# An attention stage that goes from one query tile to the next without a pause between them

## What is computed

```python
def blocked_attention(q, k, v, scale):
    ...
        s = jnp.einsum('bhgqd,bhgkd->bhgqk', qblk.astype(jnp.float32), kf) * scale
        p = jax.nn.softmax(s, axis=-1)
        return jnp.einsum('bhgqk,bhkv->bhgqv', p, vf)

def odd_attend(q_c, k_c, v_c, q_d, k_d, v_d, lam_p, lam_init, subln_g, w_out):
    o_c = blocked_attention(q_c[:, :, None], k_c[:, :, None], v_c, (NOPE_C + ROPE_C) ** -0.5)[:, :, 0]
    o_d = blocked_attention(q_d, k_d, v_d, DH_D ** -0.5)
    ...
    o_d = rms_norm(o_d[:, :, 0] - lam * o_d[:, :, 1], subln_g) * (1.0 - lam_init)
    return jnp.concatenate([from_heads(o_c), from_heads(o_d)], axis=-1) @ w_out
```

## Time and profile before

| | |
|---|---|
| median of three runs | 1700.18 us (1693.54 to 1701.67) |
| the profiled execution | 1704.54 us |
| its span, first to last instruction | 1702.8 us |
| mean granted TensorE clock | 0.891 of full speed |
| busy: PE, DVE, ACT, POOL | 79%, 31%, 20%, 10% of the span |
| layer 1: attention's units, projection, start of the expert weights | 1164.5 to 1303 us, to 1354.6 us |

### The profile page before, as it was taken

The page is one execution under the profiler, slowest core; times in us unless marked ns, Lnnn a source line. Parts: engine busy times, 40 slices in busy tenths (PEclk is TensorE's granted clock), DMA queues, the critical chain, the costliest instruction groups (busy, mean ns, idle before and its releaser), DMA issues.

```text
span 1702.8 us, 38641 instructions
## 1 busy us (share of the span) xinstructions
PE 1347.7 (79%) x16696; PEld 912.1 (54%) x16696; DVE 525.0 (31%) x1181; ACT 339.7 (20%) x702; POOL 165.9 (10%) x242
## 2 busy tenths in 40 slices
PE   4978859988998579489977748977788939986783
PEld 2457724457878244379844424444455429973441
DVE  1233331235444343411101014545455440111013
ACT  2132201032222102200100013433443220100001
POOL 1012310013333000100000012010000010000001
PEclk9999969999999779689999988986789959999997
DMA  9664162320000550949999966114330185999995
GB/s 384 258 201 138 51 249 99 148 100 3 3 3 4 209 206 0 373 157 398 391 396 403 407 244 250 50 64 149 111 137 1 60 338 216 398 392 396 395 417 190
DMA packets 42713, 357.00 MB, mean 210 GB/s; under 512 B 5755, under 2 KB 10699, under 8 KB 24272
## 3 DMA queue, kind: packets, MB, share of 16 engines
q1 hardware_dynamic: 21456, 302.11, 44.8%
q0 software_dynamic: 9312, 30.85, 5.6%
q10 hardware_dynamic: 11808, 22.03, 4.1%
HBM read 323.95 MB, written 31.01 MB: 208 GB/s over the span
## 4 chain that ended last, share of the span: by engine, by line
PE 65%; DMA 19%; DVE 8%; issue 3%; ACT 3%; SPq 1%; POOL 1%; ACTq 0%; DVEq 0%; POOLq 0%
PE PB L622 59%; DMA arena<-in_w_moe 14%; PE PB L625 5%; DVE arena L1783 5%; DMA ring<-in_w_mod 3%; ACT arena L1366 1%; DMA arena<-expert_out,rows_i 1%; DVE arena L1790 1%; POOL dispatched L565 1%; DMA arena<-in_rw_g 1%; DVE small L1796 1%; DMA dispatched<-arena,rows_i 1%; SPq L398 0%; DMA arena<-dispatched 0%; DVE x L1783 0%
## 5 line engine op out<-in xcount | busy, mean ns | idle before, releaser
L622 PE MATMUL PB<-arena 64*64 64x64 f32 (+6 forms) x9378 | 481.7, 299 | 95.0 <-DMA arena<-in_w_moe 39.5
L622 PEld LDWEIGHTS PB<-arena 64*64 64x64 f32 (+3 forms) x9378 | 377.4, 132 | 187.0 <-issue 80.0
L622 PE MATMUL PB<-ring,hT 128*128 128x512 f32 (+1 forms) x720 | 316.3, 596 | 6.2 <-DVE hT L1786 3.6
L622 PE MATMUL PB<-ring,arena 128*32 128x256 f32 (+2 forms) x3648 | 215.4, 392 | 35.8 <-DMA ring<-in_w_moe 34.3
L622 PEld LDWEIGHTS PB<-ring,hT 128*128 128x128 f32 x720 | 138.9, 196 | 168.5 <-issue 165.0
L625 PE MATMUL PB<-cst,arena 128*128 128x128 f32 (+2 forms) x790 | 128.1, 303 | 124.7 <-DMA arena<-dispatched 49.7
L622 PEld LDWEIGHTS PB<-ring,arena 128*32 128x32 f32 x3648 | 158.6, 113 | 84.7 <-DMA ring<-in_w_moe 40.7
L625 PEld LDWEIGHTS PB<-cst,arena 128*128 128x128 f32 (+2 forms) x790 | 97.4, 159 | 168.3 <-issue 103.8
L1366 ACT ACTIVATE arena<-PB 128x256 f32<-128x256 f32 (+5 forms) x222 | 104.3, 470 | 416.7 <-PE PB L622 351.6
L2163 DVE TENSOR_TENSOR arena<-arena,PB 128x256 f32<-128x256 f32 (+1 forms) x32 | 15.1, 472 | 362.9 <-ACT arena L1612 362.9
L622 PE MATMUL PB<-ring,scT 128*32 128x512 f32 x384 | 68.5, 857 | 38.6 <-DMA ring<-in_w_mod 38.6
(11 more groups left out here) (140 smaller groups left out, 899.9 us busy)
## 6 DMA issues: line engine op xcount, KB each, us to landing
ring<-in_w_moe SPq DMA_DIRECT2D x48, 2048.0 KB, 15.3
arena<-in_w_moe SPq DMA_DIRECT2D x48, 2048.0 KB, 18.4
ring<-in_w_mod SPq DMA_DIRECT2D x24, 2048.0 KB, 8.1
ring<-in_w_mix SPq DMA_DIRECT2D x22, 2048.0 KB, 8.0
dispatched<-gate ACTq DMA_DIRECT2D x1, 8320.0 KB, 39.9
arena<-dispatched POOLq DMA_DIRECT2D x20, 256.0 KB, 9.1
arena<-dispatched POOLq DMA_DIRECT2D x12, 384.0 KB, 4.0
expert_out<-gate ACTq DMA_DIRECT2D x1, 3456.0 KB, 15.6
```

The costliest lines, as they stand in the source:

```text
L622: return nc.tensor.matmul(out, lhsT, rhs, start=start, stop=stop, **k)
```

## The change

`mix` becomes two buffers, used by the tile's parity: the old one and the first half of `sq2`, which is free during attention. The exceptions of unit 15 go: `values`, `weights_T` and `out` of units 15 and 31 run one unit late like all others, behind the first unit of the next tile. The norm is cut in two: `squares(t)` on DVE after `out` in step 16 (and 32), `root` on ACT after step 17's (33's) Exp and copy, `subnorm(t)` on DVE after `out` in step 17 (33); `1 - LAM_INIT` is multiplied into the four reciprocals instead of the 512 columns. PE's transposes and DVE's copies of the tile come at the end of step 19 (35). For tile 2, `squares` and `subnorm` follow unit 47, PE transposes after the second projection block of tile 0, and DVE copies between `diagonals` and the first residual.

```diff
--- before.py
+++ after.py
@@ -265,11 +265,11 @@
         qup = u0.rearrange("p (k n) -> p k n", k=2)
         prob = take(2 * 384).rearrange("p (b n) -> p b n", b=2)
         probT = take(2 * 384).rearrange("p (b k n) -> p b k n", b=2, k=3)
-        mix = u0[:, 0:1024]
 
         hds = [hd, prob.rearrange("p b n -> p (b n)")]
         hqs = [hd2, probT.rearrange("p b k n -> p (b k n)")]
         sq2 = take(2 * D).rearrange("p (b n) -> p b n", b=2)
+        mix = [u0[:, 0:D], sq2[:, 0, :]]
 
         SCORES = (0, 1, 6, 7)
         head_items = [("k", kt) for kt in range(4)] + [("q", t) for t in range(TILES)]
@@ -710,6 +710,8 @@
                         seen[("outp", l, n)] = ("pe", count["pe"])
                         if j == 0 and n == 0:
                             spread_gates(l, 0)
+                        if l and j == 0 and n == 1:
+                            odd_mixed_T(2)
                         if j and n == 0:
                             norm(l, 1, (order[l][j - 1],))
                         if j and n == 1:
@@ -1221,6 +1223,9 @@
                     ins = tp(PB[:, b, 128 * h:128 * h + 128], src(h))
                 ins.then_inc(*tick("pe", out + "_p", t))
 
+            def odd_mixed_T(t):
+                mixed_T(("omix1", t), lambda k: mix[t % 2][:, 128 * k:128 * k + 128], t, 1)
+
             def attend():
                 units = [(t, m) for t in range(TILES) for m in range(16)]
 
@@ -1269,17 +1274,16 @@
                         scores(u + 2)
                         scores(u + 3)
                     turn(u)
-                    if u % 16:
+                    if u:
                         values(u - 1)
                     if u in mods_units:
                         for h in range(2):
                             mod_rows(*mods_units[u], h, 5)
                     if u - 2 in mods_units:
                         mod_columns(*mods_units[u - 2], 5, 0)
-                    if u % 16 == 15:
-                        values(u)
-                        t = u // 16
-                        mixed_T(("omix1", t), lambda k: mix[:, 128 * k:128 * k + 128], t, 1)
+                    if u in (19, 35):
+                        odd_mixed_T(u // 16 - 1)
+                values(47)
 
             pe.wait_ge(*when("scT"))
             for n in range(EARLY_MODS):
@@ -1735,12 +1739,12 @@
                         scale = (96 if m < 8 else 64) ** -0.5
                         fn(prob[:, u % 2, 0:n], PB[:, SCORES[u % 4], 0:n], ACT.Exp, "prob", u,
                            bias=small[:, 64 + u % 4:65 + u % 4], scale=scale, accum_out=small[:, 240 + u % 4:241 + u % 4])
-                        if m:
+                        if u:
                             weights_T(u - 1)
-                        if m == 15:
-                            weights_T(u)
-                        if m == 15:
-                            root("dd", u // 16)
+                        if u in (17, 33):
+                            root("dd", u // 16 - 1)
+                    weights_T(47)
+                    root("dd", 2)
                 gate_rows(l, 0)
                 end("act", f"mixer{l}")
                 for t in order[l]:
@@ -2036,6 +2040,8 @@
 
             def residual(l):
                 diagonals(l, 0)
+                if l:
+                    mixed(1, 2)
                 for j, t in enumerate(order[l]):
                     cond = 0 if t == 0 else 1
                     for n in range(2):
@@ -2340,14 +2346,28 @@
                     rec = small[:, 68:69]
                     step(V.reciprocal(rec, small[:, 240 + u % 4:241 + u % 4]))
                     if m < 8:
-                        ts(mix[:, 64 * m:64 * m + 64], PB[:, 4 + u % 2, 0:64], rec, None, ALU.mult, None, "ov", u)
+                        ts(mix[t % 2][:, 64 * m:64 * m + 64], PB[:, 4 + u % 2, 0:64], rec, None, ALU.mult, None, "ov", u)
                         return
-                    o = mix[:, 512 + 128 * ((m - 8) // 2):640 + 128 * ((m - 8) // 2)]
+                    o = mix[t % 2][:, 512 + 128 * ((m - 8) // 2):640 + 128 * ((m - 8) // 2)]
                     if m % 2 == 0:
                         ts(o, PB[:, 4 + u % 2, 0:128], rec, None, ALU.mult, None, "ov", u)
                     else:
                         tt(rec, rec, small[:, 62:63], ALU.mult)
                         stt(o, PB[:, 4 + u % 2, 0:128], rec, o, ALU.mult, ALU.add, "ov", u)
+
+                def squares(t):
+                    od, tmp = h8(mix[t % 2][:, 512:1024], 4), h8(hd[:, 0:512], 4)
+                    tt(tmp, od, od, ALU.mult)
+                    red(small[:, 0:4], tmp)
+                    ts(small[:, 0:4], small[:, 0:4], 1.0 / 128, EPS, ALU.mult, ALU.add, "var", "dd", t)
+
+                def subnorm(t):
+                    od, r = h8(mix[t % 2][:, 512:1024], 4), small[:, 0:4]
+                    dve.wait_ge(*when("root", "dd", t))
+                    step(V.reciprocal(r, r))
+                    ts(r, r, 1.0 - LAM_INIT, None, ALU.mult, None)
+                    tt(od, od, bc(r, 2, 128), ALU.mult)
+                    tt(od, od, bc(R(rowsO, "diff_subln_g"), 1, 4), ALU.mult, "omix1", t)
 
                 top(0)
                 top(1)
@@ -2356,15 +2376,17 @@
                         mod_chunk(*mods_units[u - 3], 5)
                     if u + 2 < 48:
                         top(u + 2)
-                    if u % 16:
+                    if u:
                         out(u - 1)
-                    if u % 16 == 15:
-                        out(u)
-                        t = u // 16
-                        od = h8(mix[:, 512:1024], 4)
-                        head_norm(od, h8(hd[:, 0:512], 4), 4, 128, R(rowsO, "diff_subln_g"), "dd", t)
-                        ts(od, od, 1.0 - LAM_INIT, None, ALU.mult, None, "omix1", t)
-                        mixed(1, t)
+                    if u in (16, 32):
+                        squares(u // 16 - 1)
+                    if u in (17, 33):
+                        subnorm(u // 16 - 1)
+                    if u in (19, 35):
+                        mixed(1, u // 16 - 1)
+                out(47)
+                squares(2)
+                subnorm(2)
 
             step(V.memset(scT[:, :], 0.0), "scT0")
             step(V.memset(zeros, 0.0), "zeros")
```

## The result

The changed kernel took 1683.56 us (median of 7 runs, 1680.67 to 1686.18) beside 1701.67 us for the kernel before (7 runs, 1693.54 to 1704.66): a ratio of 0.9901, 95% interval 0.9874 to 0.9928. By the medians that is a gain of 18.1 us and of 9.4 us; by the two intervals together, anything from 6 to 21 us. 1680 was predicted.

The account below looks back on a forecast made before the run. TensorE was taken as the bound until the experts, idling at three norm pauses. Savings of 9.3, 6.5 and 8.1 us less 3.6 for the clock gave 20.3 us: 1684.2 for the profiled execution, 1680 us as median, range 1671 to 1690.

Parts of the forecast that it names:

- The stall: TensorE before turn(18), and likewise turn(34): a new wait of 2.3 us for ScalarE's root, copy, table load and Exp.
- The drain's rival: ScalarE's table switches on each turn's path also drain, stall grows some 2.6 us: 15.1 us saved, 1685 us; 3 in 100.
- The bank wait: End of step 19: next scores wait for VectorE's copies to free banks 6 and 7; 0.45 us, bounds 0 and 1.4.
- The last tile: Tile 2 into the projection: TensorE no longer waits before the first block; 8.1 us saved.
- The clock: Work behind the stall at each turn may run slower: 1.8 us a turn taken, 3.6 us for both.
- the two turns: From tile 0 to 1 and tile 1 to 2: 9.3 and 6.5 us saved, before the clock's cost.
- the upper bound of 5.2: Most a fallen clock could cost per turn, from turn(18) to the scores of 22 and 23: 5.2 us.
- the sign named in advance: Would show the forecast wrong: granted clock 0.5 in units after 18 and 34 for longer than 6 us each.
- The experts: After the projection: they start earlier and all that follows moves along; first weights issued between 1331 and 1335.
- Slower through the clock: Rival: the stall at unit 18 drops the clock, units keep it down; 34 us cost, 1710 us; 3 in 100.
- Absorption by the experts: Rival: the experts' transfers, not the projection, set the end and absorb the gain; 1700 us; 5 in 100.
- a projection that gives its part back: Rival: late xn or diagonals make TensorE wait at each tile, losing all 8.1 us; 1688 us; 5 in 100.

Follow-up runs that it names:

- e3: Changed kernel with the last tile's transposes and copies moved back before the projection, leaving only the two turns changed; 1693.65 us, ratio to before 0.9977.
- e5: The changed kernel run again without any edit, beside the kernel before; 1688.65 us beside 1698.03, ratio 0.9937.
- e8: e2 without its one-column Exp, so the load back to Exp's table comes behind the modulation copy again; 1676.66 us, ratio to before 0.9868.
- e1: Changed kernel with three spare TensorE products before turn(18) and turn(34), filling the 2.34 us idle time; 1673.37 us, ratio to before 0.9845.
- e2: Changed kernel with root moved before chunk 21's (37's) modulation copy, a one-column Exp behind it, subnorm and transposes four steps later; 1673.49 us, ratio to before 0.9855.
- e6: e2 with one spare 96x384 TensorE product before each of turn(2), turn(6) and turn(10) in tile 0; 1662.30 us, ratio to before 0.9773.
- e9: e2 run again unchanged, beside e10 and e11 on the same chip; 1671.22 us, ratio to before 0.9833.
- e10: e6 run again unchanged, on the same chip as e9; 1670.23 us, ratio to before 0.9819.
- e11: e2 with one spare 96x384 product before the turn behind every modulation chunk in all three tiles; 1663.57 us, ratio to before 0.9792.

## Why the prediction was right, and where not

The total came out where it was forecast, 1683.6 and 1688.7 us for 1680 in a range of 1671 to 1690, but partly by luck: the clock took some 7 to 8 us more than was set down for it, and in the first pair of profiles 9.1 us that the change doesn't touch made up for them. Point by point:

- **The stall.** Forecast 2.3 us, measured 2.34 at both turns in all three profiles of the changed order (the changed kernel, e3, e5); `turn(18)` at T + 9.1 for T + 9.5, `turn(34)` at T' + 9.2 for T' + 9.9. The chain was the one named: squares, root, copy, load back, Exp. e8 priced the load's place at 1.2 to 1.3 us, as the sum had it. The drain's rival falls: in the rows above each load starts 0.01 to 0.02 us behind the operation ahead of it, and the next operation as close behind the load. The Trainium skill, "ScalarE: Activation LUTs", section "What ACT_TABLE_LOAD costs", puts a drain beside the load; it does not show on this path.
- **The bank wait.** Forecast 0.45 us. In the changed kernel it is nothing, because the transposes ran at the lower clock and VectorE's copies kept up; with the clock up, in e1, it is 0.41.
- **The last tile.** Forecast 8.1 us, measured 8.0, with both margins thinner than reckoned, though neither cost anything: the first diagonal was there at 1290.25, and `spread_gates` started at 1290.28, 6.96 us after the first block, with no wait (0.2 us of room was forecast); tile 0's `xn` was ready at 1308.78 and its transposes started at 1308.83 (0.3 forecast), as VectorE's timeline of the changed kernel shows:

```profile
1301.61 1.42 DVE L1797 COPY hT<-PB 128x512 f32<-128x512 f32 x2 [9.21 <-PE PB L625]
...
1308.03 0.75 DVE L1791 TENSOR_SCALAR arena<-x,small 128x1024 f32<-128x1024 f32 x1
```

- **The clock.** This is the term that was mis-sized: 1.8 us a turn, argued from 2.34 us being nearer to 0.63 than to 6.5. Without it the two turns were reckoned right: 93.9 us less 9.3 and 6.5 is 78.1 from T to P, and e1, with the stall in place and the clock up but for 3.4 us, has 78.6. But of the 9.3 and 6.5, 4.0 and 0.3 were left in one profile, 2.5 and 3.1 in the other. So the clock took 10.2 to 11.5 us of the two, not 3.6, and in three of the four turns it took more than the upper bound of 5.2: 5.3, 6.2, 6.8 and 3.4. The bound priced the work up to unit 23's scores, but the clock stayed low on to the second chunk:

```profile
1204.00:1217.00 13.00, 13.00 (x57) 0.50 0.13 54
1249.00:1266.00 17.00, 17.00 (x74) 0.52 0.15 64
```

  That was the sign named in advance, a clock of 0.5 for longer than 6 us. e1 shows the cause: with TensorE kept at work through the same stall, 5.7 and 5.3 us come back. What the sum missed is that the slow work behind a pause doesn't go with the pause: 9.3 and 6.5 us count it as gone, and only a third of a fall was set against that. But the clock fell at every turn again, and with no pause left to lie in, nearly all of its low time met work.
- **The experts.** They moved along: the same 348.1 us from E to the end. The first weights were issued at 1333.26, inside the 1331 to 1335 named, but 9.1 us of that were tile 0's clock and an earlier start, neither of them the change's. In the second profile of the same kernel the issue stands at 1339.02.
- **The rivals.** Slower through the clock had the fall right and its length wrong: it needed 40 us of low clock in tiles 1 and 2, and there were 27 to 31, because the same units brought the clock back 10 to 17 us after each fall. It cost a third of that rival's 34 us. Absorption by the experts and a projection that gives its part back are excluded by the stretches.

## What to carry to other kernels

Where the units around a removed pause are short, price the stall that is left not by its length but by what TensorE's clock does behind it: here 2.3 us of idle time cost 2.3 and then some 5 more. Don't count the slow work behind a pause as saved with the pause, and look how much of the low clock lay inside it, where it cost nothing. If a stall can't be moved, spare products in it are worth a try: here the stretches became 5 us shorter each. And a table load costs next to nothing (0.1 us) beside another engine's long work, but its whole length, 1.2 to 1.3 us, if it lands between a copy and the Exp behind it; a one-column activation of the wanted table draws the load to where there is room.

## What the runs showed of the hardware

- The granted clock fell behind brackets of 2.34 us six times out of six in the three profiles of the changed turns (0.80 to 0.88 over each stretch), at the latest 1.2 us after the bracket's end, and behind 1.92 us once out of two. With no bracket over 0.73 us it fell three more times in the twelve stretches of e1, e2, e6, e9, e10 and e11, for 3.4 to 7 us; ahead of e10's fall TensorE had been busy for 7.98 of 8 us. Why it falls there is open. Two executions of one program can differ by 5 us in one tile through this alone, and one profile cannot tell such a difference from a change's.
- Once it had fallen, it stayed down through 13 and 17 us (0.50 and 0.52 in the windows above) in which TensorE was busy without a gap.
- Spare products in the short stalls of tile 0 are not shown to do anything: with the same three, tile 0 took 30.5 us at 0.85 in e11 but 33.0 and 32.9 at 0.76 in e6 and e10, and 33.1 was the best without.
